# Order of the merge's first two columns, the last layer norm, and the last expert's down weights in a hybrid decoder step

## What is computed

```python
g = jax.nn.sigmoid(gates).reshape(B, T, N_BRANCH, D_MODEL)
merged = (g[:, :, 0] * (o_a @ p['p_a']) + g[:, :, 1] * (o_b @ p['p_b'])
          + g[:, :, 2] * (o_m @ p['p_m']))
return merged @ p['w_o'], ...
```

```python
y = (xf - mu) * lax.rsqrt(var + LN_EPS) * g + b
```

## Time and profile before

| what | value |
|---|---|
| median of 3 runs | 1317.51 us (1314.8 to 1317.7) |
| the profiled execution: its own time | 1323.6 us |
| its span, first to last instruction | 1321.8 us |
| TensorE busy | 1133.8 us (86%) |
| vector busy | 432.0 us (33%) |
| ScalarE busy | 238.1 us (18%) |
| HBM read, written | 277.11 MB, 24.23 MB |
| mean granted TensorE clock | 0.958 |

### The profile page before, as it was taken

One profiled execution on the slowest core, in us unless ns is written; L12 is line 12 of the kernel. 1 busy time (PEld: TensorE's weight loads), 2 busy tenths in 40 slices (PEclk: granted clock), 3 DMA queues, 4 the chain that ended last, 5 costly groups with the idle time before them and its releaser, 6 DMA issues.

```text
span 1321.8 us, 21992 instructions
## 1 busy us (share of the span) xinstructions
PE 1133.8 (86%) x9315; PEld 792.9 (60%) x9315; DVE 432.0 (33%) x824; ACT 238.1 (18%) x413; POOL 98.7 (7%) x92
## 2 busy tenths in 40 slices
PE   7999989999899999999899944999877777777775
PEld 4888866777678888877774533455444444444432
DVE  5200003576555676524342245111111111111116
ACT  4000011234621111121110110121111111111102
POOL 0400000000000000000001100111111111111110
PEclk9999998899999999999999955999999999999998
DMA  9342242312221101242638064999999999999974
GB/s 332 124 137 64 79 143 63 89 49 72 56 53 56 50 27 46 64 157 75 244 110 336 32 282 178 387 420 425 421 422 425 422 423 424 424 423 422 423 295 194
DMA packets 53346, 293.04 MB, mean 222 GB/s; under 512 B 9995, under 2 KB 12109, under 8 KB 41738
## 3 DMA queue, kind: packets, MB, share of 16 engines
q1 hardware_dynamic: 48098, 283.55, 55.3%
q0 software_dynamic: 5184, 8.54, 1.7%
HBM read 277.11 MB, written 24.23 MB: 228 GB/s over the span
## 4 chain that ended last, share of the span: by engine, by line
PE 60%; DMA 25%; DVE 5%; SPq 4%; ACT 2%; issue 2%; DVEq 1%; POOL 0%; POOLq 0%; ACTq 0%
PE psum L717 57%; DMA arena<-in_e_down 19%; DVE arena L1536 3%; SPq L673 3%; PE psum L722 3%; DMA arena<-in_e_up 3%; ACT arena L1291 1%; DMA arena<-scratch_x,arena 1%; DMA arena<-in_p_abm 1%; DVE arena L1539 1%; DVEq L1571 0%; DMA arena<-in_w_mem_kv 0%; DMA arena<-in_w_in 0%; DMA arena<-scratch_ya 0%; SPq L661 0%
## 5 line engine op out<-in xcount | busy, mean ns | idle before, releaser
L717 PE MATMUL psum<-arena 64*64 64x64 f32 (+9 forms) x8808 | 1068.4, 337 | 151.9 <-DMA arena<-in_e_gate 31.8
L717 PEld LDWEIGHTS psum<-arena 64*64 64x64 f32 (+3 forms) x8808 | 738.5, 152 | 459.4 <-issue 218.8
L1291 ACT ACTIVATE arena<-psum 128x512 f32<-128x512 f32 (+11 forms) x144 | 88.1, 635 | 657.1 <-PE psum L717 393.6
L1536 DVE TENSOR_TENSOR arena<-arena,psum 128x256 f32<-128x256 f32 (+3 forms) x136 | 74.6, 548 | 342.5 <-PE psum L717 202.7
L1536 DVE TENSOR_TENSOR arena<-arena 128x1024 f32<-128x1024 f32 (+16 forms) x173 | 133.7, 784 | 33.5 <-PE psum L717 8.7
L722 PE MATMUL psum<-arena 128*128 128x128 f32 (+5 forms) x507 | 74.8, 281 | 22.1 <-DMA arena<-scratch_x,arena 8.1
L722 PEld LDWEIGHTS psum<-arena 128*128 128x128 f32 (+5 forms) x507 | 54.8, 145 | 54.6 <-issue 32.1
L1536 DVE TENSOR_TENSOR arena<-psum,arena 128x256 f32<-128x256 f32 (+4 forms) x85 | 47.0, 564 | 68.6 <-PE psum L717 64.4
L2186 POOL TENSOR_TENSOR arena<-arena 128x1024 f32<-128x1024 f32 (+1 forms) x10 | 27.2, 2733 | 469.0 <-DVE arena L1536 469.0
L2127 DVE COPY arena<-arena 128x1 uint32 (+1 forms) x32 | 4.9, 154 | 153.9 <-PE psum L717 153.9
L2231 POOL DMA_INDIRECT arena<-scratch_x,arena x32 | 32.7, 1023 | 283.0 <-DVE arena L2118 242.0
(11 more groups left out here) (114 smaller groups left out, 200.1 us busy)
## 6 DMA issues: line engine op xcount, KB each, us to landing
arena<-in_e_gate SPq DMA_DIRECT2D x32, 2048.0 KB, 36.9
arena<-in_e_up SPq DMA_DIRECT2D x32, 2048.0 KB, 36.9
arena<-in_e_down SPq DMA_DIRECT2D x21, 2048.0 KB, 36.8
arena<-in_w_in SPq DMA_DIRECT2D x46, 512.0 KB, 3.9
arena<-in_e_down SPq DMA_DIRECT2D x44, 512.0 KB, 34.4
scratch_gates<-arena SPq DMA_DIRECT2D x24, 260.0 KB, 4.1
arena<-scratch_gates SPq DMA_DIRECT2D x8, 780.0 KB, 4.5
arena<-in_p_abm SPq DMA_DIRECT2D x8, 640.0 KB, 5.7
```

The costliest lines, as they stand in the source:

```text
L717: return pe.matmul(out, a, b, start=start, stop=stop)
L1291: return act.activation(out, a, ACT.Copy)
L1536: return v.tensor_tensor(out, a, b, op)
```

## The change

The change has four parts. On TensorE and vector, the attention products of column 1 and their gating move behind column 0's last branch, with other PSUM banks and other waits. The last layer norm is written out without the lag: vector subtracts the mean and multiplies by the gain in one pass, and multiplies by the reciprocal root and adds the bias in a second; ScalarE only takes the root. The last expert's down weights are loaded by two transfers of 1 MB, the second counted on `out_in`, and the last down product waits for the second ahead of its third chunk. GpSimd loads its register (the overflow count) ahead of the last scatter.

```diff
 sync:
-            down_load(NE - 1, (NE - 2) % 3, NE - 4)
+            sp.wait_ge(s["y_mm"], NE - 1)
+            sp.dma_start(ed[0][:, 0:2, :], wd[NE - 1][:, 0:2, :]).then_inc(s["ew0d_in"], 16)
+            sp.dma_start(ed[0][:, 2:4, :], wd[NE - 1][:, 2:4, :]).then_inc(s["out_in"], 16)
 tensor:
             gate_tile(G_MERGE + 1, (G_MERGE + 1) % 2, (G_MERGE + 1) // 2, 6)
-            pe.wait_ge(s["mgw1_in"], 32)
-            for g in (1, 2):
-                pe.wait_ge(s["proj_used"], g)
-                project(1, g, 2 * (g - 1))
             pe.wait_ge(s["head_recip"], 2)
             pe.wait_ge(s["gate_out"], G_MERGE + 2)
...
-            pe.wait_ge(s["proj_used"], 3)
+            pe.wait_ge(s["proj_used"], 1)
             gate_tile(G_MERGE + 2, (G_MERGE + 2) % 2, (G_MERGE + 2) // 2, 0)
             pe.wait_ge(s["oa_ready"], 1)
-            for q in range(2):
-                project(q, 0, 4 + 2 * q)
+            project(0, 0, 4)
+            pe.wait_ge(s["mgw1_in"], 32)
+            pe.wait_ge(s["proj_used"], 2)
+            project(1, 1, 2)
+            pe.wait_ge(s["gate_out"], G_MERGE + 3)
+            project(1, 2, 0)
+            project(1, 0, 6)
...
-            def down(q):
+            def down(q, half_in=None):
                 for k in range(FF // P):
+                    if half_in and k == 2:
+                        pe.wait_ge(s["out_in"], half_in)
...
-            down_step(NE - 1, (NE - 2) % 3, (NE - 2) // 3)
+            down_step(NE - 1, 0, (NE - 2) // 3, 96)
 scalar:
-            layer_norm(x1, 2, 1, tail=True)
+            for u in range(Q):
+                t = tile_at(2, u)
+                n = rows(t)
+                act.wait_ge(s["ln_stats"], 2 * Q + u + 1)
+                act.activation(rstd[0:n, t, :], mv[0:n, t, 1:2], ACT.Sqrt, bias=eps[0:n, 0:1]).then_inc(s["ln_std"], 1)
 vector:
-            attention_branches(0)
+            v.wait_ge(s["gate_sig"], 1)
+            for g in (1, 2):
+                v.wait_ge(s["proj_made"], g)
+                gated(0, 0, g, 2 * (g - 1), g == 1)
             v.wait_ge(s["head_root"], 2)
             v.reciprocal(rn[0:HA, :], rn[0:HA, :]).then_inc(s["head_recip"], 1)
-            attention_branches(1)
             for j in range(NJ):
...
-            for o in range(2):
-                v.wait_ge(s["proj_made"], 5 + o)
-                gated(o, o, 0, 4 + 2 * o, False)
-                v.sem_inc(s["merged"], 1)
+            v.wait_ge(s["proj_made"], 3)
+            gated(0, 0, 0, 4, False)
+            v.sem_inc(s["merged"], 1)
+            v.wait_ge(s["gate_sig"], 2)
+            for n, (g, b) in enumerate(((1, 2), (2, 0), (0, 6))):
+                v.wait_ge(s["proj_made"], 4 + n)
+                gated(1, 1, g, b, n == 0)
+            v.sem_inc(s["merged"], 1)
...
-            layer_norm(x1, 2, expert_sum, 1, tail=True)
+            for u in range(Q):
+                t = tile_at(2, u)
+                n = rows(t)
+                expert_sum(t, u)
+                src = bank(2 * t, D) if t < NT else x1[0:B, NT, :]
+                for h in range(2):
+                    v.bn_stats(st6[0:n, t, h, :], src[:, h * 512:(h + 1) * 512])
+                v.drain()
+                v.bn_aggr(mv[0:n, t, :], st6[0:n, t, :, :]).then_inc(s["ln_stats"], 1)
+                v.drain()
+                stt(x1[0:n, t, :], src, mv[0:n, t, 0:1], gb[0:n, 0, :], ALU.subtract, ALU.mult)
+                v.wait_ge(s["ln_std"], 2 * Q + u + 1)
+                v.reciprocal(rstd[0:n, t, :], rstd[0:n, t, :])
+                v.drain()
+                stt(x1[0:n, t, :], x1[0:n, t, :], rstd[0:n, t, :], gb[0:n, 1, :], ALU.mult, ALU.add).then_inc(s["x_normed"], 1)
 gpsimd:
             scatter(NE - 2, 0)
+            n_extra = extra_count(g)
             scatter(NE - 1, 1)
...
-            extra_blocks(g, extra_rows)
+            extra_blocks(g, extra_rows, n_extra)
```

More of the change, by code:

```diff
@@ L431, in tile_at, with extra_count, extra_blocks @@
             return (t - 1) % Q if pas else t
-        def extra_blocks(eng, body):
-            n = eng.value_load(ovfi.bitcast(I32)[0:1, XB:XB + 1], min_val=0, max_val=XB)
+        def extra_count(eng):
+            return eng.value_load(ovfi.bitcast(I32)[0:1, XB:XB + 1], min_val=0, max_val=XB)
+        def extra_blocks(eng, body, n=None):
+            n = extra_count(eng) if n is None else n
             with eng.If(n > 0):
@@ L1221, in turn_h_step, with down_step @@
                 turn_h()
-            def down_step(e, q, n):
+            def down_step(e, q, n, half_in=None):
                 pe.wait_ge(s["hT_ready"], e + 1)
@@ L1227, in down_step @@
                 pe.wait_ge(s["yb_ready"], e + 1)
-                down(q)
+                down(q, half_in)
             def steady(e, j, i, last=False):
@@ L1293, in _, with layer_norm @@
             eps = const("eps")
-            def layer_norm(x, pas, lag, before=None, after=None, tail=False):
+            def layer_norm(x, pas, lag, before=None, after=None):
                 scaled = s["x_scaled" if pas == 0 else "ln_scaled"]
@@ L1307, in layer_norm @@
                         act.wait_ge(s["ln_rs"], pas * Q + u + 1)
-                        src = bank(2 * i, D) if tail and i < NT else x[0:n, i, :]
+                        src = x[0:n, i, :]
                         act.activation(x[0:n, i, :], src, ACT.Identity, bias=nmr[0:n, i, :],
@@ L1544, in ts, with layer_norm @@
                 return v.tensor_scalar(out, a, s1, s2, op0, op1)
-            def layer_norm(x, pas, before, lag, tail=False):
+            def layer_norm(x, pas, before, lag):
                 for t in range(Q + 2 * lag):
@@ L1569, in layer_norm @@
                         tt(x[0:n, i, :], x[0:n, i, :], gb[0:n, 0, :], ALU.mult).then_inc(s["ln_gained"], 1)
-                        if tail:
-                            v.drain()
-                            tt(x[0:n, i, :], x[0:n, i, :], gb[0:n, 1, :], ALU.add).then_inc(s["x_normed"], 1)
             for t in range(Q + 2):
```

## The result

The changed kernel takes 1309.14 us (median of 6 runs, 1306.29 to 1311.12) against 1316.3 for the kernel before in the same session (6 runs, 1314.08 to 1319.73). The ratio is 0.9937 [0.992, 0.9953], so the change saves 8.3 us, with an interval of 6.2 to 10.5; the forecast was 9.7.

What follows compares the result with a forecast made beforehand. Chains of waits bound merge and tail, with full weight queues between. Merge 5.9, halves 0 and tail 3.8 sum to 9.7 us, to 1313.9; that execution being 6.1 above the median gave 1307.8, range 1302.5 to 1313.5.

Steps and rivals of the forecast that it cites:

- Column 2's weights in time: Merge: column 2's load is usable 1.05 us ahead of need, so TensorE's 4.26 us idle and 1.8 of half clock go.
- Column 4's load late next: Merge: column 4's load leaves TensorE 0 to 0.5 us of idle, taken as 0.2.
- Waits of the broadcasts: Merge, TensorE: waits of 0.7 ahead of the broadcasts and 0.45 at the fourth, 1.15 against 0.73, so 0.4 us lost.
- The dip: Merge: the half-clock stretch at the broadcasts, costing 2.0 us, was assumed to recur.
- rival A: Merge: half clock at the broadcasts does not recur; savings of 7.9 + 3.8, to 1305.8 us; chance 0.25.
- The weights follow the merge: Weight stream after the merge: its loads wait for the chain, so the merge's saving, 5.9 us, moves the whole stream.
- rival B: Weight stream: it hides the merge's gain, leaving the tail's 3.8 us alone, to 1313.7 us; chance 0.09.
- Halves, nothing: Last down product: splitting its weight load gains 0, as its turned input is as late as the weights.
- The register load, 0.7: Tail, GpSimd: loading the register ahead of the last scatter takes 0.7 us off the chain.
- The passes: Last norm, vector: passes of 1.22 and 1.27 us, 4.3 a tile against 4.19; the order gains, not the passes.
- The tail, 3.8: Tail: vector ends at 1314.95 against 1318.75, 3.8 us saved, the register load's 0.7 included.
- C: Merge: TensorE stays at 1.2 GHz from the broadcasts until column 1 ends; slower, 1325.3 us; chance 0.04.

Runs made afterwards that it cites:

- merge_alone: The kernel before with only the new order of TensorE's and vector's work in the merge's first two columns; ratio 0.9969 to the kernel before.
- small_alone: The kernel before with only the last down weights in halves and GpSimd's early register load; ratio 1.001 to the kernel before.
- norm_alone: The kernel before with only the last norm in two passes; ratio 0.9974 to the kernel before.
- full_rows: The changed kernel with the broadcast products reading all 128 partitions, the 120 added ones meeting zero weights; ratio 0.99 to the kernel before.
- early_first: The changed kernel with the wait for the freed bank ahead of the second broadcast instead of the first, still 8 rows; ratio 0.991 to the kernel before.
- the pieces: The changed kernel with the down weights of the expert ahead of the last also counted in two halves; ratio 0.9927 to the kernel before.
- all three edits: The changed kernel with 128-partition broadcasts, the moved broadcast wait and the last two experts' down weights in halves; ratio 0.9894 to the kernel before.

## Why the prediction was right

The predicted 1307.8 is 1.3 us below the median; 9.7 us were forecast and 8.3 measured, and 9.7 lies inside the interval of what was saved. Some of the nearness is luck: in the pair of traces the merge gave 1.2 less than its term, the tail 0.5 more, and another 1.2, which no term names, came between column 4 and the last down product (4.67 to 4.98 + 0.85); and the median of the kernel before is 1316.3 over six runs, not the 1317.5 over three that the forecast started from. By its steps:

- **Column 2's weights in time**: right. Idle 4.26 to none, and no half clock in columns 2 and 3. The load was needed at the end of column 1 and had landed by 624.95. Column 3's sigmoid starts at 634.39, so that load made it too, as forecast.
- **Column 4's load late next**: right in kind. 0.48 of idle against 0.2 forecast.
- **Waits of the broadcasts**: 0.79 ahead of them against 0.7. The 0.45 at the fourth is 0.32 in merge_alone, and nothing in the profiled execution, where the products ran at half clock and took longer than vector.
- **The dip, "I let it recur"**: it does, and this is the term that was mis-sized. It was put at 2.0 us and cost 3.7 in the profiled execution. The merge therefore gave 4.67 there and not 5.9: 1.7 more for the dip, 0.45 less for the wait that didn't come and 0.3 more of idle make 1.55, where 1.25 are missing; the 0.3 between them was not taken apart. Where the dip was short, in merge_alone, the merge gave the 5.9. As both lengths come with either order, which one a trace has is chance, and not something that the prediction could have read from the diff.
- **Its cause**: the prediction named the few-row products and the gaps together and said that the dip agrees with a page's rule on short idles (the Trainium skill, "TensorE: Matmul & The Clock Gate", section "A second HAM failure mode: psum-queue depth-cycling"). The runs don't bear out that the idles suffice. Full rows with the same waits of 0.79 and 0.32 keep 1.00 throughout; 8 rows without the 0.79 fall. Over all traces, 7 kernels of 7 with 8-row broadcasts show 0.50 at them or just behind, and 0 of 3 with full rows. The few rows are what the prediction had right; the section's rule on short idles doesn't explain this dip by itself. Nor does that page's rule on long idle, which stood behind rival A (the Trainium skill, section "HAM oscillation — how this bites in real kernels"): the clock fell with no idle above 0.8 us near.
- **The weights follow the merge**: right. The stream starts 4.98 earlier relative to the gate tile, so rival B falls: the full queues move as a whole.
- **Halves, nothing**: right, and for the reason given. The product starts 0.05 us sooner behind the one ahead.
- **The register load, 0.7**: 0.8 between the scatter's landing and the read-back. It counts only where the chain goes through the expert rows, as in the changed kernel's trace; in small_alone it did not, and the ratio shows nothing.
- **The passes**: 1.28 each against 1.22 and 1.27, 4.28 a tile against 4.3. The prediction's claim that the gain is in the order holds: the sample tile's last steps no longer stand behind tiles 0 and 1, and from the expert rows to the end it takes 24.20, where it was 27.47. That tile 0 no longer waits for TensorE is so in this trace, and not in all (0.42 in norm_alone, 1.84 in full_rows).
- **The tail, 3.8**: 4.29 between the two profiled executions. From D to vector's end, the two kernels with neither edit of the tail take 40.17 and 42.77 (mean 41.5); the four with both, leaving the pieces out, 35.88, 39.04, 36.91 and 36.84 (mean 37.2). That is 4.3 again, with a spread that no single pair of traces would show. What the prediction left out is the second path, the residual rows; where it is the later one, it sets vector's tile 0. The norm alone measured 3.4 by its ratio.
- **Rivals A and C**: A, no dip, didn't come about; the dip is there in every trace with 8-row broadcasts. C, half clock until column 1 ends, needed 19.4 us more of it than before; the longest dip seen is about 7.

The parts add up within the noise: merge alone times norm alone is 0.9969 x 0.9974 = 0.9943, and the change has 0.9937, with each ratio good to about 0.0017.

What stays open: why the dip is 3.3 to 4 us long in some executions and 6 to 7 in others of the same order (before against norm_alone and small_alone, which share the merge; merge_alone against the changed kernel). Nor was a number of rows between 8 and 128 tried, or 8 rows without any wait, and whether column 2's half clock in the kernel before came from its 4.26 us of idle alone was not taken apart.

## What to carry to other kernels

When a load is late because the buffer it fills is freed late, it can be cheaper to finish the first user's products than to make the transfer faster: here moving 24 products gave the load 40 products (8.8 us) to land under, where it had 16 (3.5 us), and cost nothing in instructions. Look at the granted clock around products that read few partitions; giving them all 128 with zero weights cost no time of its own (the first 12 took 3.06 us with 128 in full_rows and 3.05 with 8 in merge_alone) and here took away a stretch of half clock. Where several inputs of a product arrive together, bringing one forward gains nothing, and where two paths end close together (here the expert rows and the residual rows), shortening one only makes the other the last.

## What was not expected of the hardware

- TensorE fell to half clock with 16 products of 8 rows among full ones, and not on short waits alone: the 0.79 and 0.32 with full rows, the 0.48 ahead of column 4 in the changed kernel and the 0.99 there in early_first are all followed by 1.00.
- Identical work ahead of the gate tile took from 598.5 to 606.4 us over the ten traces, with granted clocks such as 0.87 and 0.96 in the same window. One pair of traces can be 7 us apart before the first changed instruction.
- The time from the last down product to vector's first pass on the expert rows, which the scatter and its read-back set, ran from 11.7 us (changed kernel, 1265.56 to 1277.24) to 13.7 (all three edits, 1264.21 to 1277.91). Vector's wait for TensorE ahead of tile 0, which the read-back of the residual rows sets, ran from none (changed kernel) to 1.84 (full rows) among the kernels with the new norm. These two make the spread of the tail.
